# Weighted sums of cached values: from GpSimd to VectorE, two 1024-column operations a page

## The reference

```python
z = jnp.einsum('bqhd,bkhd->bhqk', q, k) * SB_SCALE + sb_bias
log_keep = jnp.where(causal, jax.nn.log_sigmoid(-z), 0.0)
after = lax.cumsum(log_keep, axis=3, reverse=True) - log_keep
a = jnp.where(causal, jnp.exp(jax.nn.log_sigmoid(z) + after), 0.0)
return jnp.einsum('bhqk,bkhd->bqhd', a, v)
```

## Time and profile before

| what | us |
|---|---|
| median of 3 runs | 2712.76 |
| lowest and highest | 2712.74, 2714.4 |
| the profiled execution, its time | 2719.28 |
| its span, first to last instruction | 2717.6 |
| TensorE busy in the span | 2561.6 |
| VectorE busy | 1367.9 |
| ScalarE busy | 781.9 |
| GpSimd busy | 444.3 |

### The profile page before, as it was taken

One profiled execution on the slowest core, in us unless ns is written; L12 is line 12 of the kernel. 1 busy time (PEld: TensorE's weight loads), 2 busy tenths in 40 slices (PEclk: granted clock), 3 DMA queues, 4 the chain that ended last, 5 costly groups with the idle time before them and its releaser, 6 DMA issues.

```text
span 2717.6 us, 47590 instructions
## 1 busy us (share of the span) xinstructions
PE 2561.6 (94%) x20588; PEld 2525.8 (93%) x20588; DVE 1367.9 (50%) x1384; ACT 781.9 (29%) x912; POOL 444.3 (16%) x290
## 2 busy tenths in 40 slices
PE   7997777978799999999999999999999999999999
PEld 6997777868689999999999999999999999999999
DVE  6368878887765653343434333434243433336433
ACT  5533334535342332212121212121122222124221
POOL 3005546776631210000000000000000000003000
PEclk9999888989899999999999999999999999999999
DMA  4245554544433222222222222222222222222223
GB/s 187 95 171 191 189 191 166 188 170 157 139 117 113 86 91 94 94 94 94 81 91 94 94 94 94 94 80 99 87 94 94 94 79 94 94 94 78 99 90 109
DMA packets 57383, 309.08 MB, mean 114 GB/s; under 512 B 7770, under 2 KB 7770, under 8 KB 30178
## 3 DMA queue, kind: packets, MB, share of 16 engines
q1 hardware_dynamic: 47826, 272.50, 29.1%
q0 software_dynamic: 9216, 33.56, 3.7%
q10 hardware_dynamic: 144, 0.01, 0.0%
HBM read 297.46 MB, written 8.59 MB: 113 GB/s over the span
## 4 chain that ended last, share of the span: by engine, by line
PE 83%; DVE 13%; ACT 2%; DMA 1%; issue 1%; SPq 0%; DVEq 0%; ACTq 0%
PE out_ps L1212 79%; DVE w_lo L867 3%; DVE k_ring L898 2%; PE pair_ps L1251 1%; DVE dot_s L899 1%; DMA q_rows<-q_rows_dram 1%; DVE soft_s L925 1%; DVE z L954 1%; DVE k_third L898 1%; DVE x_lo L876 1%; DVE y L891 0%; DVE keep L952 0%; DVE keep L956 0%; PE tok_ps L1319 0%; DVE vg L1058 0%
## 5 line engine op out<-in xcount | busy, mean ns | idle before, releaser
L1212 PE MATMUL out_ps<-x_hi,w_hi 128*128 128x260 f32 x5184 | 1071.7, 288 | 29.9 <-DVE x_lo L876 10.4
L1212 PE MATMUL out_ps<-x_hi,w_lo 128*128 128x260 f32 x5184 | 1052.9, 285 | 0.0
L1212 PE MATMUL out_ps<-x_lo,w_hi 128*128 128x260 f32 x5184 | 1052.4, 285 | 0.0
L1212 PEld LDWEIGHTS out_ps<-x_hi,w_hi 128*128 128x128 f32 x5184 | 813.3, 191 | 38.5 <-issue 12.4
L1212 PEld LDWEIGHTS out_ps<-x_hi,w_lo 128*128 128x128 f32 x5184 | 808.7, 191 | 0.0
L1212 PEld LDWEIGHTS out_ps<-x_lo,w_hi 128*128 128x128 f32 x5184 | 808.2, 191 | 0.0
L867 DVE TENSOR_TENSOR w_lo<-w_raw,w_hi 128x1024 fp32r<-128x1024 f32 x410 | 535.9, 1339 | 122.6 <-ACT w_hi L610 120.9
L610 ACT ACTIVATE w_hi<-w_raw 128x1024 fp32r<-128x1024 f32 x412 | 411.7, 1047 | 548.8 <-PE out_ps L1212 548.8
L1212 PE MATMUL out_ps<-act_hi,w_lo 128*128 128x260 f32 x1408 | 283.9, 283 | 0.0
L1212 PE MATMUL out_ps<-act_lo,w_hi 128*128 128x260 f32 x1408 | 283.3, 283 | 0.0
L1212 PE MATMUL out_ps<-act_hi,w_hi 128*128 128x260 f32 x1408 | 283.2, 282 | 0.0
(11 more groups left out here) (174 smaller groups left out, 1480.4 us busy)
## 6 DMA issues: line engine op xcount, KB each, us to landing
w_raw<-w_units SPq DMA_DIRECT2D x205, 1024.0 KB, 4.9
v_ring<-cache_v POOLq DMA_DIRECT2D x64, 512.0 KB, 3.8
k_ring<-cache_k SPq DMA_DIRECT2D x50, 512.0 KB, 4.9
k_third<-cache_k SPq DMA_DIRECT2D x14, 512.0 KB, 4.0
h<-x_t SPq DMA_DIRECT2D x4, 1040.0 KB, 9.3
y_t<-h SPq DMA_DIRECT2D x16, 260.0 KB, 6.1
q_rows<-q_rows_dram SPq DMA_DIRECT2D x8, 512.0 KB, 5.4
h<-x_t SPq DMA_DIRECT2D x2, 1560.0 KB, 9.8
```

The lines of the kernel that those rows point to most:

```text
L1212: mm = pe.matmul(out_ps[:, 2 * (t % 2) + a, 0:HALF], w[:, u % 2, cols], x[:, a * HALF:(a + 1) * HALF], start=first and n == 0, stop=last a ...
```

## The change

`add_page` moves from GpSimd's program to VectorE's. Its instructions stay the same, on the same tiles: 8 products into `acc`, 56 products in place and 56 additions, all of 1024 columns. VectorE carries them out at the end of a period, behind the scores. A sample's 8 pages lie in periods `REDUCE_END[b]` - 2 to `REDUCE_END[b]`, two, three and three of them. GpSimd keeps the loads of the pages, in a list by period, and its sums of squares. The ring of values keeps its two slots.

```diff
+V_FIRST = [REDUCE_END[b] - 2 for b in range(SAMPLES)]
+
+
+def v_period(j):
+
+    b, pg = divmod(j, PAGES)
+    return V_FIRST[b] + (0, 0, 1, 1, 1, 2, 2, 2)[pg]
...
-            jobs = [(SUM_END[j // PAGES] + 1 + j % PAGES * 0.25, "page", j) for j in range(N_PAGES)]
+            jobs = [(v_period(j) - 1, "load", j) for j in range(RING, N_PAGES)]
...
+            def add_page(j):
+
+                b, pg = divmod(j, PAGES)
+                dve.wait_ge(v_in[j % RING], 16 * (j // RING + 1))
+                if pg == 0:
+                    if b == 0:
+                        dve.wait_ge(q_rows_out, 16)
+                    else:
+                        dve.wait_ge(o_s_ready, b)
+                    dve.wait_ge(a_s_done, b + 1)
+                else:
+                    dve.wait_ge(v_used, j)
+                values = v_ring[:, j % RING, :].rearrange("p (h d) -> p h d", h=HEADS)
+                weights = a_s[:, b % 3, pg * HEADS:(pg + 1) * HEADS].unsqueeze(2).to_broadcast([P, HEADS, P])
+                if pg == 0:
+                    ins = dve.tensor_tensor(acc[:, :].rearrange("p (h d) -> p h d", h=HEADS), values, weights,
+                                            ALU.mult)
+                else:
+                    chained(dve.tensor_tensor(values, values, weights, ALU.mult))
+                    ins = dve.tensor_tensor(acc[:, :], acc[:, :], v_ring[:, j % RING, :], ALU.add)
+                ins.then_inc(v_used, 1)
...
                 while pages:
                     score_next()
+                for j in v_pages(u):
+                    add_page(j)
```

More of the change, by code:

```diff
@@ L126, with v_pages @@
 CELLS = 1280
+V_FIRST = [REDUCE_END[b] - 2 for b in range(SAMPLES)]
+def v_period(j):
+    b, pg = divmod(j, PAGES)
+    return V_FIRST[b] + (0, 0, 1, 1, 1, 2, 2, 2)[pg]
+def v_pages(period):
+    return [j for j in range(N_PAGES) if v_period(j) == period]
 def k_pages(period):
@@ L527, in load_v @@
                     .then_inc(v_in[j % RING], 16)
[L529 to L549, removed]
             def add_squares(x, total, cols, done=pool_step):
@@ L569, in _ @@
             for _, kind, i in sorted(jobs):
-                if kind == "page":
-                    add_page(i)
+                if kind == "load":
+                    load_v(i)
                 elif kind == "mlp":
```

## The result

The changed kernel takes 2721.31 us (median of 12 runs, 2715.82 to 2728.41) against 2713.68 us for the kernel before (12 runs). The ratio is 1.0024 with a 95% interval of 1.0017 to 1.0032: slower by 7.6 us. The forecast was +13 us, 2726 us. The repeat further down gives 1.0027 (1.0016 to 1.0039).

A forecast was written before the change was run, and what follows sets the result against it. VectorE was taken to pace the stretch from 227.4 to 780.3 us. Contention removed -150, instructions +150, waits +32, idle filled -26 and new idle +7 gave +13 us, so 2726 us; 8 in 10 range 2698 to 2760.

The forecast's parts named there:

- The contention that goes: VectorE instructions from 227.4 to 780.3 us: 165 us of inflation from GpSimd's work, of which 150 us is removed.
- The kept part: GpSimd's 13 remaining pairs of squares still hold up VectorE: 15 us taken, bounds 0 and 30.
- The instructions that come: VectorE gains 120 page instructions of 1.225 us, 147 us, plus 3 us between chained ones: 150 us.
- The sixteen waits: VectorE waits 2 us for each third page's load in the two-slot ring: 32 us, bounds 14 and 66.
- Idle time filled at the `take`: Pages at the end of odd periods fill VectorE's waits for a unit's result in even periods from 26: -26 us.
- New waiting for `k_head`: In odd periods VectorE waits longer for ScalarE ahead of `k_head`: 1 us for each of 7 periods, +7.
- The page sums: TensorE stops before block 3 of unit `REDUCE_END` + 1; expected covered, priced at nothing, or 16 us if not.
- the term of existing waits that stay: Loads of keys, weights and query rows keep their places on SyncE's queue, and their existing waits stay.
- The faster one: Rival: page loads arrive in time, waits 14 instead of 32 us, 2698 to 2708 us; chance 0.25.
- The late landing: Rival: key loads delay the third page's load, waits 66 instead of 32 us, +47, 2760 us; chance 0.17.
- TensorE as the bound: Rival: TensorE idles for a later `take` and half the units lose 1 to 2 us, 2739 to 2751; chance 0.1.
- the part behind the stretch: The stage after 780 us, where TensorE is busy nearly throughout, was to stay as long as now, 1937 us.

The follow-up runs named there:

- The repeat further down: The changed kernel timed again with no edit, against the kernel before: 2722.21 us, ratio 1.0027.
- the two cuts on the untouched VectorE program: Kernel before, GpSimd's products in place and additions cut to 8 columns: 2592.43 us, ratio 0.9551; cut to half their columns: 2646.18 us, ratio 0.9735.
- the kernel with only the first page moved: Changed kernel with the first of three value pages added ahead of the scores at the period's end: 2702.00 us, ratio 0.9948 to the kernel before.
- the one whose VectorE had nothing to do between two pages: Changed kernel with VectorE's 56 products in place and 56 additions cut to 8 columns: 2661.88 us, ratio 0.9805 to the kernel before.

## Why the prediction was right

*The contention that goes.* I said 165 us of inflation, 15 of it kept, 150 removed. The profile has 153.9 removed. That it comes from GpSimd's page instructions is shown by the two cuts on the untouched VectorE program. The kept part was priced at 13 to 15 us of duration; cutting the squares took 13.8 us off VectorE's busy time and gave 7.2 us of time, so in time it was half of that. Without pages on GpSimd and without squares, VectorE's other work is busy for 292.6 us, so the inflation was 161 us in all (453.5 - 292.6), beside the 165 said.

*The instructions that come.* 147 us of instructions and 3 of gaps said; 153.7 and about 5 measured. Products took 1233 ns as foreseen. Additions took 1338: eight of them lie beside squares at 1.97 to 2.27 us, a meeting that I didn't see. It follows from GpSimd's new list, where the load for a third page stands ahead of squares that are ready, and holds them until VectorE is in the middle of its pages.

*The sixteen waits.* 32 us said, 28.4 measured, in exactly 16 places, at a landing of 3.6 us. That they are on the path is shown by the kernel with only the first page moved, about -21 us.

*Idle time filled at the `take`.* -26 said, 26.3 to 3.6 = -22.7 measured.

*New waiting for `k_head`.* +7 said, +6.4 measured.

*What I left out.* Two waits that I had taken as staying went as well: for the reduced sample (`q`) 9.0 to 1.3 us, and for `w_hi` 6.2 to 1.2, together -12.7 us. I take the reason to be the same as at the `take`: VectorE arrives later than the engine that it used to wait for. The page sums do come late for TensorE, which waits 41.5 us for them in 6 places; that this would be covered and not come back to VectorE, priced at nothing, held: its waits for a unit's result and for the reduced sample are shorter than before. The wait ahead of `keep_head` grew by 1.8 us, from 9.1 to 10.9. With these, and about 5 us of gaps between the added instructions, the sum becomes 28.4 - 22.7 + 6.4 - 12.7 + 1.8 + 5 = +6 us, beside +4.3 for the stretch in this pair of profiles (+7.2 in the second pair) and +7.6 us in the timed runs. So the mechanism was right, and the term of existing waits that stay was mis-sized by 13 us: I priced it at nothing. That the sum comes as near to the timed difference as it does is partly luck, since the stretch alone varies by 3.6 us between two profiles of the kernel before.

*The rivals.* The faster one decided at a wait below 1.2 us; it was 1.8 us, so it didn't come about. The late landing happened in one place, 3.35 us in period 30, and not throughout. The sixteen waits lie between 0.8 and 3.35 us; the four below 1 us (periods 18, 24, 34 and 36) are ones where the second page's addition beside the squares covers part of the wait. The periods of three pages last 19.5 to 27.9 us, where 20 to 25 was said. TensorE as the bound: its clock in the two stretches is 0.84 and 0.91, the same as before, and its result is waited for less.

*What the two spans don't show, and what stays open.* The spans of the two profiled executions (2717.6 and 2717.0 us) don't show the 7.6 us: the part behind the stretch, in which nothing was changed, is 7.4 us shorter in the profile of the changed kernel (1929.9 against 1937.3 us), and I had said that it would stay. Some 5 us of it are TensorE's clock (an estimate, added up from the granted clock of stretches of 10 us). In both profiles of the kernel before, TensorE pauses for about 1.9 us at 1330, 1890 and 2170 us (in the first one), and in the next 10 us the granted clock is 0.86 to 0.88, so partly at the lower of its two levels:

```profile
1320.00:1330.00 10.00, 10.00 (x86) 10.00 (x85) 4.63 (x6) 2.01 (x2) 0.00 (x0) 1.00 0.25 97
1330.00:1340.00 10.00, 8.06 (x65) 7.86 (x65) 4.28 (x5) 2.00 (x2) 0.00 (x0) 0.97 0.34 108
1340.00:1350.00 10.00, 10.00 (x75) 10.00 (x75) 0.17 (x1) 0.00 (x0) 0.00 (x0) 0.86 0.30 107
```

The profile of the changed kernel has a pause of 1.5 us at 1340 us and stays at 1.00 after it; its second profile loses about 2 us in this way. Why the clock falls in one kernel's profiles and hardly in the other's stays open. Even with this taken out, the pairs of profiles differ by about +4.5 and +1.2 us only. The profiled executions of the changed kernel (2718.57 and 2715.6 us) are among its faster ones, those of the kernel before (2719.28 and 2717.81) among its slower ones, so the slowdown of 7.6 us rests on the timed runs.

## What to carry to other kernels

Before you move elementwise work off GpSimd, look for instructions on VectorE that take several times their usual length while GpSimd works; the move removes that, and if the work costs as much on VectorE as the contention did, as here (154 us against 154), the time hardly changes. What decided here is where the moved work stands: put behind everything else in each period, it waited for its own ring of two slots; put into the waits that VectorE has anyway, the same instructions gave 1.5%. An existing wait for an engine is no constant: once the waiting engine gets more work, it shrinks, and it should stand in the sum with both ends.

## What the runs showed of the hardware

In this kernel GpSimd's work held up VectorE's roughly in proportion to the length of GpSimd's instructions, and dearly: halving the columns took 111 us off the two lines of page instructions (268.5 us in the earlier trace rows, 157.6 then) and brought 71.6 us of time, and cutting them to 8 columns brought 122.5. An eight-column addition of VectorE, 167 ns by itself, averaged 467 ns beside them. Not every instruction of VectorE was held up. The score's product, which reads two tiles in SBUF, took 1763 ns beside the pages and 1269 without them; the reduction right behind it, with one tile of the same size as its input, took 1220 ns in both kernels (the first row before, the second after):

```profile
L899 DVE TENSOR_REDUCE dot_s<-k_ring 128x8 f32<-128x1024 f32 x40 | 48.8, 1220 | 1.4
L890 DVE TENSOR_REDUCE dot_s<-k_ring 128x8 f32<-128x1024 f32 x40 | 48.8, 1220 | 1.4
```

Nor did work with one input in PSUM change (`z<-z,pair_ps`: 1211 and 1216 ns; `y<-out_ps,x_r`: 696 and 692). One input alone is no protection, though: the `TENSOR_SCALAR` `vg<-vg,lnb` took 1678 ns beside the pages and 491 in the changed kernel.

How a pair of squares cost only about 1 us each can be read in period 18 above. VectorE's addition beside it began at 307.52 and ended at 309.51 us, 1.10 us after the end of GpSimd's product (308.41); GpSimd's addition had begun at 308.49 and ended 1.13 us after VectorE's. That fits the two engines taking turns instruction by instruction, so that VectorE waits for one of the pair and GpSimd for VectorE; it is a reading of these rows, and no run tested it.

The landing time of a 512 KB page was 3.6 us in the median in the changed kernel, 4.6 us in the one whose VectorE had nothing to do between two pages, and 4.7 us in the kernel before with GpSimd's page instructions cut to 8 columns.
